# A two-layer hybrid decoder step on one core: memory norm inside the projection, token norm beside the memory products, and four convolution chunks on TensorE

## The reference

```python
# every layer: cross-attention into 256 memory tokens
kv = rmsnorm(mem, P['norm_mem'][l]) @ P['w_xkv'][l]            # memory keys and values
x = x + cross_attn(rmsnorm(x, P['norm_x'][l]), mk, mv, l, P)
# layer 1: convolution module
u = h @ P['w_pw1'][o] + P['b_pw1'][o]
glu = u[..., :D_CONV] * jax.nn.sigmoid(u[..., D_CONV:])
y, new_buf = causal_dwconv(buf0, glu, P['w_dw'][o])            # depthwise, 31 taps, 1024 channels
y = jax.nn.silu(layernorm(y + P['b_dw'][o], P['ln_g'][o], P['ln_b'][o]))
out = y @ P['w_pw2'][o]
```

## Time and profile before

| | us |
|---|---|
| median of three runs | 4378.6 (4378.32 to 4379.95) |
| the profiled execution | 4383.36 |
| its span (first to last instruction) | 4381.8 |
| PE busy | 3797.5 (87%) |
| DVE busy | 1671.5 (38%) |
| POOL busy | 1296.2 (30%) |
| ACT busy | 701.2 (16%) |
| projection to query product, layer 0 | 1439.6 to 1548.3 |
| convolution, VectorE's first to last pair | 2708.5 to 3001.8 |
| projection to query product, layer 1 | 3155.3 to 3261.4 |

### The profile page before, as it was taken

The page is one execution under the profiler, slowest core; times in us unless marked ns, Lnnn a source line. Parts: engine busy times, 40 slices in busy tenths (PEclk is TensorE's granted clock), DMA queues, the critical chain, the costliest instruction groups (busy, mean ns, idle before and its releaser), DMA issues.

```text
span 4381.8 us, 56464 instructions
## 1 busy us (share of the span) xinstructions
PE 3797.5 (87%) x22341; PEld 3455.7 (79%) x22341; DVE 1671.5 (38%) x1617; ACT 701.2 (16%) x1030; POOL 1296.2 (30%) x723
## 2 busy tenths in 40 slices
PE   6988899677768798889999998992878789999997
PEld 5766666566668697789999998942878689999997
DVE  1035488533324205242312234998311524122232
ACT  1024311111101103020101112122111212010010
POOL 1000122211104041334444444600313134444442
PEclk9899999688878898899999999995999899999998
DMA  1000145522221232311111111100141411111111
GB/s 70 29 20 0 59 150 162 104 76 77 77 110 44 67 115 91 130 39 45 47 48 44 48 48 44 48 0 2 39 149 61 165 39 39 45 47 48 45 47 58
DMA packets 77633, 282.26 MB, mean 64 GB/s; under 512 B 9113, under 2 KB 9386, under 8 KB 74066
## 3 DMA queue, kind: packets, MB, share of 16 engines
q1 hardware_dynamic: 53282, 170.22, 12.8%
q0 software_dynamic: 24240, 110.42, 7.5%
HBM read 256.88 MB, written 24.77 MB: 64 GB/s over the span
## 4 chain that ended last, share of the span: by engine, by line
PE 67%; issue 12%; DVE 12%; ACT 3%; DMA 2%; POOL 2%; SPq 1%; DVEq 1%; POOLq 0%; ACTq 0%
PE ps L464 45%; PE ps L448 3%; PE ps L509 1%; DVE wk L939 1%; PE ps L1482 1%; DVE la L427 1%; DMA w_raw<-wallb 1%; PE ps L1147 1%; PE ps L644 1%; DVE la L1854 1%; DVE h_lo L421 1%; PE ps L663 1%; PE ps L1134 1%; PE ps L1510 1%; DVE wk L941 1%
## 5 line engine op out<-in xcount | busy, mean ns | idle before, releaser
L292 POOL TENSOR_TENSOR w_hi<-w_raw,ones 128x1024 fp32r<-128x1024 f32 x192 | 466.2, 2428 | 1265.0 <-PE ps L464 1215.3
L464 PE MATMUL ps<-h_hi,w_hi 128*128 128x344 f32 x3072 | 662.8, 325 | 61.6 <-DVE h_lo L421 33.1
L464 PE MATMUL ps<-h_lo,w_hi 128*128 128x344 f32 x3072 | 658.0, 323 | 0.0
L464 PE MATMUL ps<-h_hi,w_lo 128*128 128x344 f32 x3072 | 654.5, 322 | 0.0
L464 PEld LDWEIGHTS ps<-h_hi,w_hi 128*128 128x128 f32 x3072 | 523.3, 191 | 67.8 <-issue 49.8
L293 POOL TENSOR_TENSOR w_lo<-w_raw,w_hi 128x1024 fp32r<-128x1024 f32 x192 | 558.7, 2910 | 15.1
L464 PEld LDWEIGHTS ps<-h_lo,w_hi 128*128 128x128 f32 x3072 | 526.0, 191 | 0.0
L464 PEld LDWEIGHTS ps<-h_hi,w_lo 128*128 128x128 f32 x3072 | 517.6, 190 | 0.0
L448 PE MATMUL ps<-hT,w 128*128 128x344 f32 x1152 | 340.9, 459 | 4.7 <-ACT wk L999 2.1
L464 PE MATMUL ps<-a_lo,w_hi 128*128 128x344 f32 x1536 | 325.9, 320 | 0.0
L464 PE MATMUL ps<-a_hi,w_hi 128*128 128x344 f32 x1536 | 325.8, 320 | 0.0
(11 more groups left out here) (419 smaller groups left out, 4320.8 us busy)
## 6 DMA issues: line engine op xcount, KB each, us to landing
w_raw<-wallb SPq DMA_DIRECT2D x224, 512.0 KB, 3.5
xT<-kpool POOLq DMA_DIRECT2D x128, 256.0 KB, 3.2
xT<-vpool SPq DMA_DIRECT2D x128, 256.0 KB, 2.9
xT<-cmk POOLq DMA_DIRECT2D x16, 1024.0 KB, 5.3
w<-wall SPq DMA_DIRECT2D x14, 1024.0 KB, 5.0
x_spill<-xT POOLq DMA_DIRECT2D x2, 4128.0 KB, 19.4
xT<-x_spill POOLq DMA_DIRECT2D x2, 4128.0 KB, 14.2
xT<-cmv POOLq DMA_DIRECT2D x8, 1024.0 KB, 5.4
```

Source lines behind the costliest of these rows:

```text
L292: S["pool"].link(nc.gpsimd.tensor_tensor(w_hi[:, s], w_raw[:, s], one, ALU.mult))
L464: ins = nc.tensor.matmul(ps[:, 3 * (j % 2) + n, 0:N3], wt[:, j % 2, k, :], src[:, k, n * N3:(n + 1) * N3], start=(k == 0 and n_pass == 0), ...
```

## The change

The memory norm moves into the projection ahead of `cross(l)`: `pe_product3_mem` puts its sums ahead of tile 3 and its spread ahead of tile 4, VectorE and ScalarE run its other steps between the residuals (`dve_mixed_norms`, `act_mixed_norms`). The two norms change numbers (memory 1 and 6, tokens 2 and 7), and their spreads get banks of their own. The token norm's sums and spread stand ahead of memory tiles 2 and 4 (`pe_memory`, now without loops), and ScalarE's eight passes behind its copies of tiles 4 to 11 (`act_memory`). `pe_sums`, `pe_spread`, `act_square`, `act_root`, `act_spread`, `act_hi` and `dve_root` are the steps of the old functions under names of their own. In layer 1 GpSimd loads the memory right after the layer norm, ahead of the remaining splits of `pw2`.

The convolution's chunks 4 to 7 go to TensorE, in another form; VectorE keeps chunks 0 to 3. Each of the chunks is written to memory (`spill`) and read back four times shifted by 0 to 3 tokens, each time 32 channels x 4 groups onto 32 partitions (`shifted`, tile `x4`, seven half chunks of 512 columns in the place of `h_hi` and `h_lo`). A matmul then takes four taps of 32 channels at once, 8 of them in a row give all 31 taps, and the four groups write 32 PSUM partitions each. VectorE builds the stationary tiles `d_w` ahead of its loop, in the place of masks that layer 0 alone uses. SP issues the spills and loads between the second and the third weight tile of `pw2`. Several semaphores are merged (`by_dve`, `by_pe`) with the same order of signals.

```diff
...
+            def tiles(t0, t1):
+                with sp.Fori(0, (t1 - t0) // 2) as i:
+                    for s in range(2):
+                        if s == 0:
+                            sp.wait_ge(psum_ready, GROUPS_A)
+                        sp.wait_ge(w_split, i * 2 + (s + 1 + t0))
+                        sp.dma_start(w_raw[:, s, :, :],
+                                     wallb[ds(i * 2 + (s + t0), 1)].rearrange("a p (k n) -> p (a k) n", k=KC))\
+                            .then_inc(w_loaded[s], 16)
+            tiles(0, TILE0["pw2"] + 2)
+            sp_conv(sp)
+            tiles(TILE0["pw2"] + 2, NTILES)
...
-        X_NORM, M_NORM, F_NORM = (1, 6), (2, 7), (3, 8)
-        OUT0 = {n: 8 * n for n in range(10)} | {1: 16, 2: 8, 6: 56, 7: 48}
-        SPLIT = {1: 0, 3: 1, 4: 2, 5: 3, 6: 4, 8: 5}
+        X_NORM, M_NORM, F_NORM = (2, 7), (1, 6), (3, 8)
+        OUT0 = {n: 8 * n for n in range(10)}
+        SPLIT = {2: 0, 3: 1, 4: 2, 5: 3, 7: 4, 8: 5}
+        SPREAD_AT = {1: 3584, 6: 3584, 2: 2048, 7: 2048}
...
+        def act_mixed_norms(act, l, name):
+            m, x = M_NORM[l], X_NORM[l]
+            act.wait_ge(xa["mem"], 16 * (l + 1))
+            for c in range(KC):
+                act_square(act, m, m_raw, NMEM, c)
+            for c in range(KC):
+                if c == 2:
+                    act_root(act, m, NMEM)
+                elif c == 3:
+                    act_spread(act, m, NMEM)
+                act.wait_ge(psum_free, GROUP0[name] + c + 1)
+                act_square(act, x, xT, T, c)
...
+        def dve_mixed_norms(dve, l, name):
+            m, x, g0 = M_NORM[l], X_NORM[l], GROUP0[name]
...
+            S["dve"].link(nc.vector.memset(acc, 0.0))
+            dve.wait_ge(psum_free, g0)
+            for c in range(KC):
+                dve.wait_ge(psum_ready, g0 + c + 1)
+                nc.vector.tensor_tensor(thirds(xT[:, c, :]), thirds(xT[:, c, :]), psum_set(c % 2), ALU.add)\
+                    .then_inc(psum_free, 1)
+                if c == 0:
+                    for k in range(KC):
+                        dve.wait_ge(nm_sq, 8 * m + k + 1)
...
+                dve.wait_ge(nm_sq, 8 * x + c + 1)
+                dve.wait_ge(nm_add, 8 * x + c)
+                nc.vector.tensor_tensor(acc, acc, sq[:, c % 2], ALU.add).then_inc(nm_add, 1)
+                if c == 1:
+                    dve_root(dve, m, NMEM)
+                elif c == 2:
+                    dve_scale(dve, m, m_raw, m_n, NMEM, f"norm_mem{l}")
+            dve_root(dve, x, T)
...
+        def pe_product3_mem(pe, name, l, hi, lo, wait_src):
+            t0, g0 = TILE0[name], GROUP0[name]
+            for j in range(8):
+                if j == 3:
+                    pe_sums(pe, M_NORM[l], NMEM)
+                elif j == 4:
+                    pe_spread(pe, M_NORM[l], NMEM)
+                pe.wait_ge(w_split, t0 + j + 3)
+                pe.wait_ge(psum_free, g0 + j - 1)
+                product3_tile(pe, j, hi, lo, wait_src if j == 0 else None)
...
+            t0, g0 = TILE0[f"mk{l}"], GROUP0[f"mk{l}"]
+            for t in range(16):
+                j = t % 2
+                if t == 2:
+                    pe_sums(pe, X_NORM[l], T)
+                elif t == 4:
+                    pe_spread(pe, X_NORM[l], T)
+                pe.wait_ge(w_loaded[j], 16 * (NPAIRS + (t0 + t) // 2 + 1))
+                pe.wait_ge(psum_free, g0 + t - 1)
...
+        def pool_memory(pool):
+            pool.dma_start(m_raw, memT_in).then_inc(xa["mem"], 16)
...
+                pool_memory(pool)
...
+        x4 = at("x4", ARENA - 6144 - 2 * XW, [P, 7, 4, 540])
+        d_w = [part(masks, 0, 32, 32)] + [part(la, 15296 + 1024 * n, 32, 32) for n in range(3)]
+        d_taps, d_w4, d_fold = part(masks, 1024, 4, 4, CC), part(masks, 1520, 4, 4, 8), part(masks, 1648, 32)
+        glu_spill = x_spill.rearrange("p c t -> p (c t)")
+        HW = 540
...
+            w0 = VOFF["w_dw"][0] + 4 * CC
+            for a in range(4):
+                pool.dma_start(d_taps[32 * a:32 * a + 32].rearrange("p g c t -> p g (c t)"),
+                               vecs_in[:, w0:w0 + 4 * CC].rearrange("(g p) n -> p g n", g=4)).then_inc(cm["taps"], 16)
...
+            pe.wait_ge(cm["diag"], 4)
+            for n in range(8):
+                pe.wait_ge(x4_loaded[n], 64)
+                for b in range(8):
+                    for g in range(4):
+                        ins = nc.tensor.matmul(ps[32 * g:32 * g + 32, n, :], d_w[n // 2][:, 8 * g + b, :],
+                                               x4[:, n % 7, g, 4 * b:4 * b + 512], start=(b == 0), stop=(b == 7))
+                ins.then_inc(cm["used"], 1)
+        def act_conv_out(act):
+            for n in range(8):
+                c, half = 4 + n // 2, n % 2
+                act.wait_ge(cm["used"], n + 1)
+                nc.scalar.activation(glu[:, c, half * 512:half * 512 + 512], ps[:, n, :], ACT.Identity,
+                                     bias=v("b_dw", c)).then_inc(cm["pv"], 1)
+        def sp_conv(sp):
+            def spill(c):
+                sp.wait_ge(cm["glu"], c + 3)
+                sp.dma_start(glu_spill[:, (c - 4) * GW:(c - 3) * GW], glu[:, c, :]).then_inc(cm["spill"], 16)
+            def shifted(c):
+                sp.wait_ge(cm["spill"], 48 if c < 7 else 64)
...
+                    n = 2 * (c - 4) + half
+                    if n == 7:
+                        sp.wait_ge(cm["used"], 1)
+                    for a in range(4):
+                        t0 = (c - 4) * GW + half * 512 + a
+                        wide = min(HW, GW - half * 512 - a)
+                        sp.dma_start(x4[32 * a:32 * a + 32, n % 7, :, 0:wide],
+                                     glu_spill[:, t0:t0 + wide].rearrange("(g p) t -> p g t", g=4)).then_inc(x4_loaded[n], 16)
+            for c in range(4, 7):
+                spill(c)
+            sp.wait_ge(psum_ready, GROUP0["pw1"] + 16)
+            shifted(4)
+            spill(7)
+            for c in range(5, 8):
+                shifted(c)
...
+            link = S["dve"].link
+            dve.wait_ge(cm["taps"], 64)
+            link(vv.memset(d_w4, 0.0))
+            link(vv.tensor_tensor(d_fold, strips[:, 0, :], strips[:, 1, :], ALU.add))
+            for a in range(4):
+                q, nb = slice(32 * a, 32 * a + 32), 8 if a < 3 else 7
+                for g in range(4):
+                    ins = vv.tensor_copy(d_w4[q, :, g, 0:nb], d_taps[q, g, :, a:a + 4 * nb - 3:4])
+            link(ins)
+            for n in range(4):
+                w4 = d_w4[:, n].rearrange("p g b -> p (g b)").rearrange("p (x n) -> p x n", n=1).to_broadcast([P, 32, 32])
+                fold = d_fold.rearrange("p (x n) -> p x n", x=1).to_broadcast([P, 32, 32])
+                vv.tensor_tensor(d_w[n], w4, fold, ALU.mult).then_inc(cm["diag"], 1)
...
-            with S["dve"].loop(3, 2 * 36) as i:
+            with S["dve"].loop(2, 2 * 36) as i:
...
+            for c in (4, 6):
+                for step in range(4):
+                    for h in range(2):
+                        lag(rows(c + h, h, step))
...
+                    dve.wait_ge(cm["pv"], 2 * (c + h - 4) + 2)
+                    S["dve"].link(put_rows(c + h, h))
+                dve.sem_inc(cm["out"], 2)
+            dve.wait_ge(cm["pv"], 8)
...
+            g0, x = GROUP0[f"mk{l}"], X_NORM[l]
+            act.wait_ge(psum_free, g0)
+            for t in range(16):
+                act.wait_ge(psum_ready, g0 + t + 1)
...
+                ins.then_inc(psum_free, 1)
+                if t == 1:
+                    act_root(act, x, T)
+                elif t == 3:
+                    act_spread(act, x, T)
+                elif 4 <= t < 12:
+                    act_hi(act, x, t - 4)
...
+            pool.wait_ge(nm_out, 48)
+            pool_memory(pool)
...
-            pool.wait_ge(nm_out, 48)
...
-                act_norm(act, X_NORM[l], xT, T, behind(("out", "pw2")[l]))
-                act_norm(act, M_NORM[l], m_raw, NMEM, once((xa["mem"], 16 * (l + 1))))
-                act_scale(act, X_NORM[l])
+                act_mixed_norms(act, l, ("out", "pw2")[l])
...
-            act_conv_taps(act)
+            act_conv_out(act)
...
-                dve_norm(dve, X_NORM[l], T, ("out", "pw2")[l])
-                dve_norm(dve, M_NORM[l], NMEM)
-                dve_scale(dve, M_NORM[l], m_raw, m_n, NMEM, f"norm_mem{l}")
+                dve_mixed_norms(dve, l, ("out", "pw2")[l])
...
-                pe_norm(pe, X_NORM[l], T)
-                pe_norm(pe, M_NORM[l], NMEM)
...
-                pe.wait_ge(nm_cp, M_NORM[l] + 1)
...
-            pe_product3(pe, "pw2", 2, h_hi, h_lo, by_chunk(nm_out, OUT0[5]))
+            pe_product3_mem(pe, "pw2", 1, h_hi, h_lo, by_chunk(nm_out, OUT0[5]))
...
```

More of the change, by code:

```diff
@@ L140, in build @@
         ones = sb("ones", [P, P])
[L141 to L148, removed]
+        masks = sb("masks", [P, 14 * P])
```

(27 more changed lines are left out.)

200 lines of the change are left out of this document (86 added, 114 removed).

## The result

The changed kernel takes 4227.32 us (median of 4 runs, 4219.67 to 4233.71) against 4378.46 (4 runs): a ratio of 0.9659, 95% interval 0.9637 to 0.9681. The forecast was 4249 with a range of 4230 to 4285: the direction and the places were right, the gain is 21.7 us larger than said, and the time lies just under the range. The profiled execution took 4228.0 us (span 4226.4, against 4381.8 before).

A forecast was written before the change was run, and what follows sets the result against it. TensorE's three-pass products hold most of the chain; gains come where the chain leaves TensorE. Convolution -74.3 and both projection-to-query-product crossings -55.4 give -129.7 us, from a median of 4378.6 to 4249; range 4230 to 4285.

The forecast's parts named there:

- Convolution, VectorE: Odd layer's convolution: VectorE's loop runs twice instead of three times, -74.3 us; building the stationary tiles (8 to 13 us) is hidden.
- Convolution, TensorE: Four chunks as 256 matmuls on TensorE take 55 us, done 33 us before VectorE, so they cost nothing.
- Transfers: Convolution's spills and 32 shifted loads, 8.85 MB: between 30 and 98 us, taken as under TensorE's 55 us, which hides them.
- loads late: Rival, convolution: quarter-width shifted loads move slower; 12 us less gain, or 21 at low clock, 4261 to 4270; chance 0.08.
- slower than before: Rival, convolution: shifted loads fall to 34 GB/s and take 258 us, sums 98 us late, 4421 us; chance 0.05.
- ScalarE still in the way: Rival, memory tiles: copies wait behind token passes, the 8.27 us stall returns in both layers, 16.6 us back, 4266; chance 0.11.
- Token norm beside the memory products: Projection to query product: norm steps between memory tiles make the stretch 79.7 us per layer, -55.4 us in both together.
- Sums and spread: Token norm's two TensorE steps between memory tiles: 4.00 + 4.01 us, less 0.6 us each, so 6.8 us per layer.
- The memory norm's 1.01 + 1.22: Memory norm's two sums and two spreads on TensorE inside the projection: +2.2 us per layer.
- Sixteen tiles: A layer's memory tiles on TensorE at 3.91 us each, including waits for raw weights: 62.5 us.
- The wait for GpSimd: After the last memory tile, TensorE's wait for GpSimd's first split stays, 8.19 us.
- a pair of tiles at its 7.21 us: Fast end of the crossings' range: memory tile pairs take only TensorE's own 7.21 us, -65 us for both crossings.

The follow-up runs named there:

- e8: Changed kernel with each of the 32 shifted loads turned into one of the same bytes into all 128 partitions; 4226.69 us (one run).
- e10: Kernel before with the two norms' part of the change alone, as much of it looped on TensorE as its order allows; 4300.2 us (one run).
- e6: Changed kernel with the token norm's sums and spread taken ahead of the first memory tile again, in both layers; 4246.38 us, ratio 0.9706 to the kernel before.
- e2: Kernel before with the two norms' part of the change alone, the convolution as before; 4302.24 us, ratio 0.9829.
- e5: Changed kernel once more, unchanged and loaded afresh; 4226.65 us, ratio 0.966 to the kernel before.
- e1: Kernel before with the convolution's part of the change alone, the norms as before; 4296.85 us, ratio 0.9823.
- e3: Kernel before with the 16 memory tiles of a layer written out instead of looped; 4375.12 us, ratio 0.9998.
- e4: Changed kernel with the eight value tiles of each layer in a loop of twice four again; 4230.89 us (one run).
- e9: Kernel before with memory tiles, two projections and two query products written out on TensorE, order of work as before; 4368.64 us, ratio 0.9985.

## Where the prediction was right, and the step that failed

**Convolution, VectorE: right.** 74.7 us against 74.3, and the building of the stationary tiles is hidden, at 9 us of 8 to 13. **Convolution, TensorE: right.** 57.4 us against 55, at a granted clock of 0.96 in that stretch, and 37 us of slack against 33. **Transfers: right in the effect.** The 32 loads run at the quarter-width rate, which TensorE hides; "loads late" and "slower than before" did not come. In e8 nearly doubling their rate leaves the time where it was.

**ScalarE still in the way: did not come.** Its passes lie between the copies, and no memory tile of after waits for it (one tile pair of e10 does, 0.53 us).

**Token norm beside the memory products: the step that failed, by its sizes.** The mechanism was right, and the gain is the order's own: e10 has it (crossings of 71.3 us) with the landing time of before. The sum of 79.7 us per layer, 159.4 in both, was 69.73 + 70.76 + 2 x 1.1 = 142.7, so 16.7 us of the 21.7 are here:

- Sums and spread were put at 6.8 us per layer; between the tiles they take 1.92 + 1.93. That is 5.9 us over both layers. I took 4.00 and 4.01 from the earlier trace rows without asking at which clock they were read, though TensorE had just waited there; e6 brings 3.3 to 4.0 us back by bringing the wait back. The memory norm's 1.01 + 1.22, also behind a wait, became 0.50 + 0.61: another 2.2 us.
- Sixteen tiles were put at 62.5 us; they are 58.0 and 59.1, together 7.9 us less. Some 1 to 2 us of this are the sooner landings (e10, the same order at 3.5 us, has about 59.5 in each layer, together 1.2 us more than e2 and 2.0 more than after). The rest is in the 3.91 itself. It is a mean over one stretch of before that is mostly value tiles (7.41 us a pair in flow) and has a wait ahead of nearly every pair, five of 0.27 to 0.36 us and this one of 0.96:

```profile
3226.39 7.41 PE L1422 MATMUL ps<-w_raw,la 128*128 128x128 f32 x64 [0.96 <-DMA w_raw<-wallb]
```

I gave it to the key tiles as well, which take 7.07 and 7.15 a pair next to the two steps and wait for nothing.
- The wait for GpSimd (8.07 and 8.05 against 8.2), and a first tile that starts 0.2 us ahead of the residual, are the last 0.7 us.

Of the other 5 us, 0.4 are VectorE's convolution; the rest lies outside these places and isn't settled. It isn't steady either: in e5, on another chip, the whole gain is 148.7 us, 19.0 over the 129.7, so that only 2 are left. Profiles of one kernel differ by more than that (two of before have spans of 4381.8 and 4370.6), also in places that the change leaves alone: two of after wait 3.8 and 4.8 us for the same loads (`cmv`) in the cross-attention of layer 0.

**The range.** Its fast end was "a pair of tiles at its 7.21 us", -65 for both crossings. I had the tiles' floor in it but not the clock's: the two norm steps stayed at their half-clock price in every case. With both norms' steps at the measured price (5.9 + 2.2 us less) it would have been -73; measured are -72.0.

## What to carry to other kernels

A duration read behind a wait of TensorE can be a half-clock duration (here 3.3 to 4.0 us instead of 2.06): look at the granted clock of that row's window before using it for a place in full flow, and put both prices into the range. A small step that moves off a wait can therefore gain twice, the wait and up to half of itself. And where TensorE is fed from two slots and a load takes about as long as a tile (here 3.2 to 3.5 us beside 3.5 to 3.7), a few tenths of a microsecond in the landing decide how often it waits, so take the mean of a tile from more than one stretch and for each kind of tile by itself.

## What the runs showed of the hardware that I had not expected

The landing time of the 512 KB weight loads went with the program's written-out code. In the profiles whose instruction queue moved 1.43 to 1.49 MB (before twice, e1, e3, e10) it is 3.5 us, in those with 1.54 to 1.62 MB (after twice, e2, e4, e6 to e9) 3.2 to 3.3, also far from the crossings; the page loads of 256 KB on the same queue (2.9 to 3.0 us) don't move with it. The kernel before with more code written out (e9) is 0.15% faster, part of which may be the missing loops. The cause is open, and so is whether the amount of code or its place counts.
